# mLSTM gates: the input part in plain fp32 from the unsplit tile, in TensorE's column quarters, inside the next input chunk

## What is computed

```python
E2 = 2 * D_MODEL; H = 4; DH = 512; CHUNK = 64            # D_MODEL 1024, SEQ 512, CTX_LEN 256

def mlstm_inputs(hmod, grid_rows, grid_cols, w_in, conv_w, conv_b, w_q, w_k, w_if, b_i, b_f):
    xm, o_pre, z = jnp.split(hmod @ w_in, 3, axis=-1)
    xconv = silu(depthwise_conv_3x3(xm) + conv_b)
    xh = xconv.reshape(b, n, H, DH)
    q = jnp.einsum('bnhd,hde->bhne', xh, w_q)
    k = jnp.einsum('bnhd,hde->bhne', xh, w_k) * (DH ** -0.5)
    v = xm.reshape(b, n, H, DH).transpose(0, 2, 1, 3)
    wq_g, wk_g, wv_g = (w_if[:, i].reshape(2, H, DH, 2 * H) for i in range(3))
    gates = (jnp.einsum('bhne,rheg->rbng', q, wq_g) + jnp.einsum('bhne,rheg->rbng', k, wk_g)
             + jnp.einsum('bhne,rheg->rbng', v, wv_g))
    li = gates[..., :H] + b_i
    lf = jax.nn.log_sigmoid(gates[..., H:] + b_f)
    return (q, k, v, li, lf), o_pre, z, xconv
```

## Time and profile before

| | us |
|---|---|
| median of 3 runs | 2256.07 (2256.03 to 2262.36) |
| the profiled execution | 2257.16 |
| its span | 2255.0 |
| TensorE busy in the span | 2188.2 (97%) |
| VectorE busy | 1437.1 (64%) |
| ScalarE busy | 865.0 (38%) |
| POOL busy | 1084.1 (48%) |
| mean granted clock of TensorE | 0.993 |

### The profile page before, as it was taken

How to read it: one execution, slowest core, us unless ns; L and a number is a source line. 1 busy time by engine, 2 the same in 40 slices (tenths; PEclk the granted TensorE clock), 3 DMA queues, 4 the chain that set the end, 5 groups by cost and what they waited for, 6 DMA issues and landing times.

```text
span 2255.0 us, 31166 instructions
## 1 busy us (share of the span) xinstructions
PE 2188.2 (97%) x11306; PEld 1802.2 (80%) x11306; DVE 1437.1 (64%) x2299; ACT 865.0 (38%) x1458; POOL 1084.1 (48%) x1273
## 2 busy tenths in 40 slices
PE   8999999999999999999988999999999999999998
PEld 6788877888688887788777888887787887888886
DVE  3598858764558885887678766638576776433322
ACT  3534353222553335222354433434344344333321
POOL 3565436665356544676525544432434344343443
PEclk9999999999999999999999999999999999999999
DMA  8322227663332222666313222232424333222222
GB/s 275 94 87 82 75 76 247 234 213 118 103 94 85 75 75 89 227 204 201 111 55 103 103 80 99 96 111 102 133 74 152 96 111 99 59 73 75 70 80 75
DMA packets 97576, 259.87 MB, mean 115 GB/s; under 512 B 10400, under 2 KB 20000, under 8 KB 97312
## 3 DMA queue, kind: packets, MB, share of 16 engines
q1 hardware_dynamic: 76224, 212.51, 29.4%
q10 hardware_dynamic: 21216, 45.51, 5.6%
HBM read 237.01 MB, written 20.97 MB: 114 GB/s over the span
## 4 chain that ended last, share of the span: by engine, by line
PE 54%; issue 21%; POOL 14%; DVE 7%; ACT 2%; DMA 1%; ACTq 0%; POOLq 0%; DVEq 0%
PE bank L2199 17%; PE bank L2200 17%; PE bank L2201 16%; POOL t L479 13%; DVE t L1855 3%; DVE t L1316 1%; PE bank L2436 1%; DVE t L1320 1%; PE bank L2445 1%; PE bank L2612 1%; DMA t<-w_ada 1%; PE bank L2285 0%; DVE t L1810 0%; DVE t L1852 0%; PE bank L2456 0%
## 5 line engine op out<-in xcount | busy, mean ns | idle before, releaser
L479 POOL TENSOR_TENSOR t<-t,t 128x256 fp32r<-128x256 f32 x1172 | 1005.2, 889 | 1038.8 <-ACT t L553 1038.3
L2199 PE MATMUL bank<-t,t 128*128 128x512 f32 (+1 forms) x3056 | 1170.7, 383 | 25.7 <-DVE t L1316 5.8
L2200 PE MATMUL bank<-t,t 128*128 128x512 f32 (+1 forms) x3056 | 1142.4, 374 | 0.0
L2201 PE MATMUL bank<-t,t 128*128 128x512 f32 (+1 forms) x3056 | 1141.8, 374 | 0.0
L2199 PEld LDWEIGHTS bank<-t,t 128*128 128x128 f32 x3056 | 576.0, 188 | 154.6 <-issue 11.1
L2201 PEld LDWEIGHTS bank<-t,t 128*128 128x128 f32 x3056 | 575.1, 188 | 105.3
L2200 PEld LDWEIGHTS bank<-t,t 128*128 128x128 f32 x3056 | 576.1, 189 | 103.3 <-issue 4.3
L553 ACT ACTIVATE t<-t 128x1024 fp32r<-128x1024 f32 x302 | 317.0, 1054 | 275.9 <-PE bank L2201 245.5
L1651 DVE SCALAR_TENSOR_TENSOR t<-t,t,t 128x512 f32<-128x512 f32 x240 | 217.2, 905 | 7.5 <-ACT t L735 1.0
L1382 DVE SCALAR_TENSOR_TENSOR t<-t,t,t 128x512 f32<-128x512 f32 x168 | 158.9, 965 | 43.3 <-ACT t L840 29.9
L1320 DVE SCALAR_TENSOR_TENSOR t<-t,bank 128x512 f32<-128x512 f32 x112 | 76.7, 685 | 135.8 <-ACT t L1273 59.8
(11 more groups left out here) (256 smaller groups left out, 1684.0 us busy)
## 6 DMA issues: line engine op xcount, KB each, us to landing
t<-blocks SPq DMA_DIRECT2D x306, 512.0 KB, 3.6
t<-w_ada SPq DMA_DIRECT2D x160, 256.0 KB, 4.2
t<-w_ada SPq DMA_DIRECT2D x14, 512.0 KB, 10.3
xm_park<-t ACTq DMA_DIRECT2D x16, 384.0 KB, 2.3
s_park<-t ACTq DMA_DIRECT2D x16, 384.0 KB, 2.5
t<-xm_park ACTq DMA_DIRECT2D x16, 384.0 KB, 4.8
t<-s_park ACTq DMA_DIRECT2D x16, 384.0 KB, 5.3
xc_park<-t ACTq DMA_DIRECT2D x16, 256.0 KB, 2.2
```

The costliest lines, as they stand in the source:

```text
L479: low = pool.tensor_tensor(w_lo[slot][:, part], w_raw[slot][:, part], w_hi[slot][:, part].bitcast(F32), ALU.subtract)
L2199: pe.matmul(out, wh, xh, start=start, stop=False)
L2200: pe.matmul(out, wh, xl, start=False, stop=False)
L2201: return pe.matmul(out, wl, xh, start=False, stop=stop)
```

## The change

The input part of the gates is no longer computed from split parts. `gate_x` takes the unsplit tile `xm_f[c % 2]` and plain fp32 weights `gate_v` (8 columns each for the input and the forget gates), in eight calls: the left half of the columns into rows 0 and 32 of the bank, the right half into rows 64 and 96, for the latents and then for the context. `xm_high`, `xm_parts`, xmH and xmL are gone. Each gate_x but the last and gate_x(1, 2) stands in the middle of a following chunk (`middle` in `pair`). Two matmuls with zero weights (`start_gates`) clear the two banks, in place of one `keep_busy`. gate_w and gate_v have two buffers each, gate_w is 104 columns wide, and the weights of head h + 1 are spread earlier: for head 1 within conv(0, 3), for heads 2 and 3 within the query tiles of the head before. For that the list of blocks has another order, as do the conditions under which ScalarE may reuse a block's buffer and xm_f.

The diff, cut to its core:

```diff
-        xmH, xmL = at(172 * KB, [128, SEQ], F32R), at(175 * KB, [128, SEQ], F32R)
+        gate_v = [at(172 * KB + 256 * i, [128, NC, 16]) for i in range(2)]
+        gate_zero = at(172 * KB + 512, [32, 128])
...
-        gate_w = at(188 * KB, [128, 3 * NC, 128], F32R)
+        GATE_ROWS = 104
+        gate_w = [at(188 * KB + 4 * 2 * NC * GATE_ROWS * i, [128, 2 * NC, GATE_ROWS], F32R) for i in range(2)]
@@ -297,10 +299,13 @@
-            ahead = [("x", h + 1, c) for c in ((1,) if h else (1, 2))] if more else []
             A_ORDER += [("x", h + 1, 0)] if more else []
-            A_ORDER += ahead + queries + keys if h == 0 else queries + ahead + keys
-            A_ORDER += ([("x", h + 1, 2), ("gates", h + 1), ("x", h + 1, 3)] if h else [("x", 1, 3), ("gates", 1)]) if more else []
+            if h == 0:
+                A_ORDER += [("gates", 1), ("x", 1, 1), ("x", 1, 2)] + queries + keys + [("x", 1, 3)]
+            elif more:
+                A_ORDER += queries + [("gates", h + 1), ("x", h + 1, 1)] + keys + [("x", h + 1, 2), ("x", h + 1, 3)]
+            else:
+                A_ORDER += queries + keys
@@ -539,9 +545,9 @@
-                    if b - RING == AB["gates", 0]:
+                    if b - RING in GATE_BLOCKS:
 
-                        act.wait_ge(dve_done, Dn("gate_w", 0))
+                        act.wait_ge(dve_done, Dn("gate_w", GATE_BLOCKS[b - RING]))
@@ -945,7 +951,8 @@
                     act.wait_ge(xm_parked[c % 2], 16 * (n // 2))
-                    act.wait_ge(dve_done, Dn("xmL", *divmod(n - 2, NC)))
+                    act.wait_ge(pe_done, P("gate_x", *divmod(n - 2, NC)))
+                    act.wait_ge(act_done, A("pads", *divmod(n - 2, NC)))
@@ -1015,10 +1014,8 @@
             xm_out(0, 0)
-            xm_high(0, 0)
             for c in (1, 2, 3):
                 xm_out(0, c)
-                xm_high(0, c)
                 if c == 3:
                     xm_out(1, 0)
                 pads(0, c)
@@ -1514,24 +1504,27 @@
             def spread_gates(h):
 
                 b = AB["gates", h]
                 dve.wait_ge(weights_lo, b + 1)
-                if h:
-                    wp("gate_k", h - 1, NC - 1)
+                if h >= 2:
+                    wp("gate_k", h - 2, NC - 1)
...
+                dve.tensor_tensor(gate_v[h % 2][:], parts[0][:, 2 * NC:, :], parts[1][:, 2 * NC:, :], ALU.add).then_inc(dve_done, d())
@@ -1874,14 +1863,12 @@
-            conv(0, 0, 0, 3)
-            xm_parts(0, 0)
-            conv(0, 0, 3)
+            conv(0, 0)
             for c in range(1, NC):
-                xm_parts(0, c)
                 conv(0, c, 0, 3)
                 if c == 3:
                     cd.also("last_line")
+                    spread_gates(1)
@@ -2587,13 +2561,15 @@
                 for n, s in enumerate(slots):
+                    if n == len(slots) // 2 and middle:
+                        middle()
@@ -2606,17 +2582,22 @@
-                w = gate_w[:, kt, :]
+                w = gate_w[h % 2][:, kt, :]
                 for n in range(2):
-                    pe.matmul(banks[7][:], w, lat[n], start=(first and n == 0), stop=(last and n == 1))
+                    pe.matmul(banks[7][0:GATE_ROWS, :], w, lat[n], start=False, stop=(last and n == 1))
...
+            def start_gates():
+
+
+                pe.wait_ge(dve_done, Dn("gate_zero"))
+                pe.wait_ge(dve_done, Dn(L1 - 1, "x_norm", KT - 1))
+                pe.matmul(banks[7][:], gate_zero[:], vec[0:32, 0:512], start=True, stop=False)
+                pe.matmul(banks[6][:, 0:CTX], gate_zero[:], vec[0:32, 0:CTX], start=True, stop=False)
@@ -2631,15 +2612,20 @@
             def gate_x(h, c):
-                free = [(dve_done, Dn("xmL", h, c))]
+
+                pe.wait_ge(act_done, A("xm", h, c))
                 if c == 0:
-                    free.append((dve_done, Dn("gate_w", h)))
-                gate(GV + c, (xmH[:, CTX:], xmL[:, CTX:]), (xmH[:, 0:CTX], xmL[:, 0:CTX]), ("gate_x", h, c), free)
...
+                    pe.wait_ge(dve_done, Dn("gate_w", h))
+                for bank, first, n in ((banks[7], CTX, S // 2), (banks[6], 0, CTX // 2)):
+                    for half in range(2):
+                        part = xm_f[c % 2][:, first + n * half:first + n * (half + 1)]
+                        for k in range(2):
+                            row = 64 * half + 32 * k
+                            mm = pe.matmul(bank[row:row + 8, n * half:n * (half + 1)], gate_v[h % 2][:, c, 8 * k:8 * k + 8], part, start=False, stop=False)
+                mm.then_inc(pe_done, p("gate_x", h, c))
@@ -2670,17 +2657,16 @@
             for c in (2, 3):
-                xm(0, c)
-                gate_x(0, c - 2)
+                xm(0, c, lambda: gate_x(0, c - 2))
             for h in range(MH):
                 more = h + 1 < MH
                 if more:
-                    xm(h + 1, 0)
+                    xm(h + 1, 0, lambda: gate_x(h, 3 if h else 2))
                     if h == 0:
-                        gate_x(0, 2)
-                        xm(1, 1)
-                        xm(1, 2)
-                gate_x(h, NC - 1)
+                        xm(1, 1, lambda: gate_x(0, 3))
+                        xm(1, 2, lambda: gate_x(1, 0))
+                else:
+                    gate_x(h, NC - 1)
```

More of the change, by code:

```diff
@@ L322, in program @@
         W_BANK = (0, 1, 6, 7)
-        GQ, GK, GV = 0, NC, 2 * NC
+        GQ, GK = 0, NC
+        GATE_BLOCKS = {AB["gates", h]: h for h in range(MH)}
         OUT_BANK = (7, 2)
@@ L516, in _ @@
                     for c in range(NC):
[L517 removed]
+                        if (h or c < 3) and b == ((AB["x", h, 3],) * 2 + (AB["q", h, 0], AB["q", h, 1]) if h else (AB["x", 1, 0], AB["x", 1, 1], AB["q", 0, 0], AB["q", 0, 1]))[c]:
                             pool.wait_ge(act_done, A("xcH", h, c))
@@ L957, in xm_out @@
                 split_to(AB["x", h, c] + 1 + RING)
[L959 to L965, removed]
             def pads(h, c):
@@ L1516, in clear_gates @@
                 dve.memset(line_pad[:], 0.0).then_inc(dve_done, d())
-                dve.memset(gate_w[:].bitcast(F32), 0.0).then_inc(dve_done, d("gates_clear"))
+                for w in gate_w:
+                    dve.memset(w[:].bitcast(F32), 0.0).then_inc(dve_done, d())
             def frames():
+                dve.memset(gate_zero[:], 0.0).then_inc(dve_done, d("gate_zero"))
                 dve.memset(grid_pad[:], 0.0).then_inc(dve_done, d("frames"))
@@ L1902, in _ @@
                     last_low(2).then_inc(dve_done, d("last_low"))
-                if more:
-                    xm_parts(h + 1, 0)
                 for e in range(NC):
@@ L1912, in _ @@
                         conv(h + 1, 0, 3 * e, 3 * e + 3)
+                    if more and h and e == 2:
+                        spread_gates(h + 1)
                 if more:
@@ L2587, in _, with pair @@
                     sum_quarters(banks[3], sq_t[j % 3], j == 0, j == KT - 1, (l, "x_sq", j))
-            def pair(b, slots, lat, con, bank_pair, label, free, end):
+            def pair(b, slots, lat, con, bank_pair, label, free, end, middle=None):
                 latents, context = bank_pair
@@ L2633, in xm @@
                 pair(AB["x", h, c], range(KT), lambda k: (uH[:, k, :], uL[:, k, :]), lambda k: (cH2[:, k, :], cL2[:, k, :]),
-                     X_BANK(h, c), ("xm", h, c), free, True)
+                     X_BANK(h, c), ("xm", h, c), free, True, middle)
             def gate_x(h, c):
-                free = [(dve_done, Dn("xmL", h, c))]
+                pe.wait_ge(act_done, A("xm", h, c))
                 if c == 0:
-                    free.append((dve_done, Dn("gate_w", h)))
-                gate(GV + c, (xmH[:, CTX:], xmL[:, CTX:]), (xmH[:, 0:CTX], xmL[:, 0:CTX]), ("gate_x", h, c), free)
-                if c == 0 and h:
-                    cp.also("block", AB["gates", h])
+                    pe.wait_ge(dve_done, Dn("gate_w", h))
[6 more added lines that the diff above has]
+                mm.then_inc(pe_done, p("gate_x", h, c))
             def gate_q(h, e):
@@ L2663, in _ @@
             spread(banks[5], tmp[2], ("n0",))
-            keep_busy(7, 2)
+            keep_busy(7, 1)
+            start_gates()
             for k in range(KT):
@@ L2711, in _ @@
                 if more and h:
-                    xm(h + 1, 1)
+                    xm(h + 1, 1, lambda: gate_x(h + 1, 0))
                 for e in range(NC):
@@ L2719, in _ @@
                 if more:
-                    xm(h + 1, 2 if h else 3)
+                    xm(h + 1, 2 if h else 3, lambda: gate_x(h + 1, 1))
                 gate_k(h, NC - 1)
@@ L2731, in _ @@
                     mm.then_inc(pe_done, p("scores", h, i))
-                    if more and i < 3:
-                        gate_x(h + 1, i)
-                        if i == 0 and h:
-                            xm(h + 1, 3)
+                    if more and i == 0:
+                        if h:
```

(3 more changed lines are left out.)

45 lines of the change are left out of this document (10 added, 35 removed).

## The result

| | before | changed |
|---|---|---|
| median, us | 2258.49 (2255.16 to 2262.36, 11 runs) | 2264.93 (2261.46 to 2268.43, 11 runs) |
| ratio to before | | 1.0027, 95% interval 1.0018 to 1.0037 |
| span of the profiled execution | 2255.0 | 2261.8 |

A forecast was written before the change was run, and what follows sets the result against it. TensorE was taken as the bound, busy 2188.2 of 2255.0 us. Later q(0,2) +5.2, gate_x(1,0) already paid -0.7, two gate_x waits gone -0.7, eleven gates +1.9 gave +5.7: 2261.8 us, own range 2257 to 2263, with rivals 2254 to 2267.

The forecast's parts named there:

- The sum: Whole kernel: 5.2 - 0.7 - 0.7 + 1.9 = +5.7 us, forecast 2261.8 us, 0.25% more.
- The new wait: TensorE before xm(1, 1): 9.7 us for POOL's low part, because x(1, 1) is split only after xm_out(0, 3).
- the chain through conv(0, 0): VectorE and ScalarE ahead of xm(1, 0): without one low part of 1.49 us the chain moves 1.5 us forward.
- one stretch, 1.7 us: xm(1, 1), after the new wait: one stretch of 3.4 us at half clock, costing 1.7 us.
- two stretches: Rival, xm(1, 1): idling costs two half-clock stretches, another 1.7 us, total +7.4, 2263.5 us; chance 0.25.
- The swallowed waits: TensorE on the way to q(0, 2): old waits of 2.45, 1.9 and 0.78 us disappear behind the new wait.
- The gates: Gate matmuls of x on TensorE: 0.87 us per gate_x, 0.17 more than before; 16 cost +2.7 us.
- The price of the quarters: TensorE going into the column quarters and back: 0.22 us per gate_x.
- the two waits of gate_x: TensorE at 1275.62 and 1370.35: waits of 0.30 and 0.39 us for low parts go, -0.7 us.
- The later heads: Heads 1 to 3: the new block order has slack and costs nothing; unchanged but for 0.17 us per gate.
- Narrow weights: Rival: gate_w at 104 columns loads worse, lengthening 256-column steps; +4.5 us, total +10.2, 2266.3 us; chance 0.08.
- Weights in time: Rival before q(0, 2): only VectorE's last low part holds TensorE; sum -1.3 us, 2254.8 us; chance 0.17.

The follow-up runs named there:

- the filled wait: Changed kernel with nine plain 512-column matmuls ahead of xm(1, 1), inside the 8.7 us wait; median 2261.80 us, ratio 1.0014 to the kernel before.
- the mended kernel: Changed kernel with gates 1's block ahead of x(1, 0), one split more after xm_out(0, 1 to 3), gates 1 spread before conv(0, 2); 2256.06 us, ratio 0.9993 to before.
- the kernel with the late split: Kernel before with only the split of x(1, 1) moved behind xm_out(0, 3), gates untouched; median 2261.95 us, ratio 1.0015 to the kernel before.
- the one with the parts put back: The mended kernel with xm's 16 high and 16 low parts back at their old places, written to an unread tile; 2258.81 us, ratio 1.0002 to before.
- The last kernel: The pairs, with only the first 256 columns of a gates' block split and made low; median 2252.51 us, ratio 0.9974 to the kernel before.
- the pairs: The mended kernel with twelve of the sixteen gate_x taken two at a time; median 2256.22 us, ratio 0.9987 to the kernel before.
- The wide kernel: The mended kernel with each gate_x as two plain fp32 calls on 40 rows over all columns, not eight in quarters; 2265.37 us, ratio 1.0030 to before.

## Why the prediction was right

- **The sum.** +5.7 us was forecast, +6.1 measured by the ratio (4.1 to 8.4 by its interval), +6.1 in the stage of the two profiles.
- **The new wait.** Named by its place, its releaser and its cause from the two orders of ScalarE, and shown by undoing it. Forecast 9.7 us, measured 8.7. Its end was right (49.15 us into the stage; the forecast 1196.9 is 49.4): the split of x(1, 1) came at 44.0, as forecast (43.9), POOL took 3.85 us, not 4.36, and TensorE started 0.15 us behind it. Its beginning was later than forecast, 40.4 us, not 39.7: the chain through conv(0, 0) came forward by 1.1 us at xm(1, 0), not 1.5 (VectorE's ten instructions there took 10.37 us, against 1.31 + 8.68 before), and xm(1, 0) with its gate took longer.
- **The clock.** The step "one stretch, 1.7 us" was too small: 5.1 us of work ran at half clock and xm(1, 1) took 11.83 us, 2.6 more than the 9.26 forecast without it; the filled wait gives 2.4. The stretch did not begin about 1 us after the work came back, as in the earlier trace rows, but 5 us before, and lasted some 10 us; only half of it fell on work. The rival "two stretches" asked for more than 5.6 us of work at half clock and did not come about, by 0.5 us.
- **The swallowed waits.** None before q(0, 0) to q(0, 2): the steps from 70.33 to 78.73 are 8.4 us. The last low part ended at 1223.3, 75.0 us into the stage, and was due at 76.6. VectorE stood for 6.0 us behind the tanh that comes after xm_out(1, 1) (L991), as foreseen.
- **The gates.** A size was off here. The price of the quarters was read up to the product at 329.68, and that product's own late step was left out: 0.31 us there and back, not 0.22, and 0.96 us a gate_x, not 0.87. Behind q(0, 2) this made the gates 11 x 0.96 - 12 x 0.70 = +2.2 us, where +1.2 was forecast. That the rest of the stage cost +0.2 us and not more than the +0.5 forecast is luck, from errors of the other sign: the two waits of gate_x that went were worth 1.2 us with the slow starts around them (0.7 forecast), the first wait of gate_q shrank by 0.4 (nothing forecast), and smaller ones give 0.4.
- **The later heads.** No new wait; what is left there (1.45, 1.45, 0.93 and 1.31 us) is what was there before.
- **The rivals.** Narrow weights: refuted. Weights in time: it is the mended kernel, forecast as -1.3 us, measured -1.6 (0.9993, an interval that holds 1). Its q(0, 2) starts 2.05 us before the old one, 1.8 forecast.

So the mechanism was right, and that the sum came within half a microsecond is in part luck: the clock was 0.7 us too low and the gates 1.2, and the waits that went or shrank, with the quicker POOL, made up for most of it.

## What to carry to other kernels

Where weights pass through a ring with a fixed order, a block put in early pushes every later block one split back, and a split's place in a queue decides, not its length: look for what stands ahead of the next split (here a convolution on another engine) before moving a block that nobody needs yet. Taking work off engines that aren't the bound paid some 2 us at most here, not clear of the noise, and one misplaced block cost 8. A wait on TensorE should be priced with the half clock behind it: of the changed kernel's excess, 2.4 to 2.9 us came back by filling the wait. After waits of 2.0 to 2.6 us it can go either way: the two in the stage of the kernel before (2.04 and 2.45 us) were followed by none, those of 2.0 us in the kernel with the late split and of 2.6 and 2.1 us in the one with the parts put back by 3.4 us of half clock each. And the price of a narrow matmul between full ones is read up to the end of the first full one behind it, not to its start.

## What was not expected

- VectorE and POOL slow each other down more than I had reckoned. In the changed kernel nine instructions of a convolution (L1844) took 9.16 us while POOL worked for 7.3 us of them, and 7.96 us while it worked for 4.4:

```profile
1177.11 9.16 DVE L1844 SCALAR_TENSOR_TENSOR t<-t,t,t 128x512 f32<-128x512 f32 x9
...
1189.94 7.96 DVE L1844 SCALAR_TENSOR_TENSOR t<-t,t,t 128x512 f32<-128x512 f32 x9
```

  With the block on POOL held back in the kernel before, nine such instructions took 7.73 us beside 3.0 us of POOL's work, and the next split came forward. The last kernel shows it too: without the three empty pieces of a gates' block, ten of them in conv(0, 0) took 10.00 us instead of 11.06 in the pairs, and xm(1, 0) started at 30.40 us instead of 31.45. No run changes POOL's load alone.
- The matmul that enters a narrow form starts 0.21 us behind a full one instead of 0.12, in quarters as with 40 columns, and the full one behind it takes 0.34 us instead of 0.23.
- The wide kernel's excess over the mended one, 8.4 us by the ratio, is more than the 6.7 us of its stage; in its profile the part behind the stage, where nothing was changed, is 3.8 us longer, with one stretch of half clock more. Why is open.
